# Attention heads in pairs: bias and mask added on VectorE with the maximum, scores four items ahead

## The reference

```python
def joint_softmax(parts, extra=None):
    m = parts[0].max(-1, keepdims=True)
    for p in parts[1:]:
        m = jnp.maximum(m, p.max(-1, keepdims=True))
    if extra is not None:
        m = jnp.maximum(m, extra)
    es = [jnp.exp(p - m) for p in parts]
    den = es[0].sum(-1, keepdims=True)
    for e in es[1:]:
        den = den + e.sum(-1, keepdims=True)
    if extra is not None:
        den = den + jnp.exp(extra - m)
    return [e / den for e in es]

def neighbourhood_attention(q, k, v, k_ctx, v_ctx, rpb):
    ...
    bias = jnp.where(col_ok[None, None, :, None, :], bias, NEG)
    s_loc = jnp.einsum('bhrqd,bhrjkd->bhrqjk', qg, kg, preferred_element_type=jnp.float32) * scale + bias
    s_ctx = jnp.einsum('bhrqd,bhld->bhrql', qg, k_ctx, preferred_element_type=jnp.float32) * scale
    p_loc, p_ctx = joint_softmax([s_loc.reshape(b, h, rows, GRID_W, kh * GRID_W), s_ctx])
    ...
    o = (jnp.einsum('bhrqjk,bhrjkd->bhrqd', p_loc, vg)
         + jnp.einsum('bhrql,bhld->bhrqd', p_ctx.astype(v.dtype), v_ctx))

def window_gqa(q, k, v, k_ctx, v_ctx, sink):
    ...
    ok = (jnp.abs(kpos - qpos) <= SWA_WINDOW) & (kpos >= 0) & (kpos < n)
    s_loc = jnp.where(ok, jnp.einsum('bkgnqd,bknmd->bkgnqm', qb, kb, preferred_element_type=jnp.float32) * scale, NEG)
    s_ctx = jnp.einsum('bkgnqd,bkld->bkgnql', qb, k_ctx, preferred_element_type=jnp.float32) * scale
    p_loc, p_ctx = joint_softmax([s_loc, s_ctx], extra)
    ...
```

## Time and profile before

| | us |
|---|---|
| median of three runs | 2750.54 |
| lowest and highest | 2749.99, 2753.0 |
| the profiled execution | 2752.89 |
| its span | 2751.1 |
| PE busy in the span | 2641.9 (96%) |
| DVE busy | 1401.4 (51%) |
| ACT busy | 571.7 (21%) |
| mean granted clock of TensorE | 0.983 |

### The profile page before, as it was taken

One profiled execution on the slowest core, in us unless ns is written; L12 is line 12 of the kernel. 1 busy time (PEld: TensorE's weight loads), 2 busy tenths in 40 slices (PEclk: granted clock), 3 DMA queues, 4 the chain that ended last, 5 costly groups with the idle time before them and its releaser, 6 DMA issues.

```text
span 2751.1 us, 38407 instructions
## 1 busy us (share of the span) xinstructions
PE 2641.9 (96%) x15510; PEld 1859.8 (68%) x15510; DVE 1401.4 (51%) x2718; ACT 571.7 (21%) x1142; POOL 545.3 (20%) x420
## 2 busy tenths in 40 slices
PE   7999999999999999999999999999999998999998
PEld 4347568888865655789964464788888756655554
DVE  2556366466758677533556542765555335410111
ACT  1215221100033334322022041100000225201110
POOL 0000034444400000047830000444454000000000
PEclk8999999999999999999999999999999998999998
DMA  8551035555333423445445400554543300499995
GB/s 299 199 185 53 31 124 199 182 179 175 110 86 99 115 74 100 152 151 179 144 128 208 145 31 32 177 188 163 168 142 113 124 1 1 171 417 412 415 404 219
DMA packets 218210, 446.71 MB, mean 162 GB/s; under 512 B 18762, under 2 KB 115849, under 8 KB 214955
## 3 DMA queue, kind: packets, MB, share of 16 engines
q1 hardware_dynamic: 176688, 329.78, 33.4%
q10 hardware_dynamic: 41338, 114.40, 12.3%
HBM read 443.01 MB, written 1.13 MB: 161 GB/s over the span
## 4 chain that ended last, share of the span: by engine, by line
PE 89%; DVE 5%; ACT 2%; DMA 1%; issue 1%; POOL 0%; SPq 0%; DVEq 0%; ACTq 0%; POOLq 0%
PE bank L1101 34%; PE bank L929 24%; PE bank L2955 5%; PE bank L953 4%; PE bank L945 3%; PE bank L2974 3%; PE bank_pair L2955 2%; PE bank L2464 1%; DMA slot<-in_ada_w 1%; PE bank L2991 1%; PE bank L2040 1%; PE bank_pair L2974 1%; PE bank L2033 1%; PE bank L2457 1%; PE bank L2928 1%
## 5 line engine op out<-in xcount | busy, mean ns | idle before, releaser
L1101 PE MATMUL bank<-arena,slot 128*128 128x256 f32 (+1 forms) x3704 | 677.0, 343 | 6.3 <-DVE arena L1081 2.9
L1101 PEld LDWEIGHTS bank<-arena,slot 128*128 128x128 f32 x3704 | 605.0, 191 | 70.5 <-issue 8.0
L1114 POOL TENSOR_TENSOR slot<-slot 128x512 f32<-128x512 f32 (+3 forms) x208 | 269.3, 1295 | 1578.5 <-PE bank L1101 699.6
L929 PE MATMUL bank<-uT,slot 128*128 128x512 f32 (+2 forms) x1312 | 484.8, 525 | 2.8 <-ACT arena L2073 2.8
L929 PEld LDWEIGHTS bank<-uT,slot 128*128 128x128 f32 (+1 forms) x1312 | 246.5, 190 | 217.2 <-issue 205.0
L1101 PE MATMUL bank<-uT,slot 128*128 128x256 f32 (+1 forms) x1728 | 335.4, 351 | 6.3 <-ACT uT L681 6.1
L1101 PEld LDWEIGHTS bank<-uT,slot 128*128 128x128 f32 x1728 | 290.7, 192 | 44.6 <-ACT uT L681 10.4
L1115 POOL TENSOR_TENSOR slot<-slot 128x512 f32<-128x512 f32 (+3 forms) x208 | 286.8, 1379 | 0.0
L929 PE MATMUL bank<-arena,slot 128*128 128x256 f32 (+1 forms) x576 | 185.2, 485 | 3.8 <-DVE arena L1762 2.3
L929 PEld LDWEIGHTS bank<-arena,slot 128*128 128x128 f32 x576 | 111.9, 195 | 75.8 <-issue 66.9
L650 DVE SCALAR_TENSOR_TENSOR arena<-arena 128x1024 f32<-128x1024 f32 x95 | 122.3, 1297 | 11.9 <-issue 8.8
(11 more groups left out here) (459 smaller groups left out, 3064.9 us busy)
## 6 DMA issues: line engine op xcount, KB each, us to landing
slot<-in_ffn_w SPq DMA_DIRECT2D x42, 2048.0 KB, 8.7
arena<-in_ada_wt ACTq DMA_DIRECT2D x100, 512.0 KB, 3.6
slot<-in_moe_w SPq DMA_DIRECT2D x62, 704.0 KB, 16.8
arena<-in_moe_w SPq DMA_DIRECT2D x52, 704.0 KB, 17.8
rstd<-in_ada_wt ACTq DMA_DIRECT2D x48, 512.0 KB, 3.6
slot<-in_moe_w SPq DMA_DIRECT2D x11, 2048.0 KB, 18.8
slot<-in_ssd_w_in SPq DMA_DIRECT2D x32, 512.0 KB, 6.9
uT<-in_ada_wt ACTq DMA_DIRECT2D x28, 512.0 KB, 3.6
```

What stands on the lines that cost most here:

```text
L929: ins = pe.matmul(bank[0:m, 0:t1 - t0], w[:, k, c0:c0 + m], x[:, k, t0:t1], start=(k == 0), stop=(k == kt - 1))
L1101: ins = pe.matmul(bank[:, u * n:u * n + n], a[:, k, u * P:u * P + P], x[:, k, :], start=(k == 0), stop=(k == self.h - 1))
L1114: pool.tensor_tensor(out[:, :, 0:c], x[:, :, 0:c], y[:, :, 0:c], op)
```

## The change

- **s**: bias and mask leave TensorE. `pair_pe` is now two products of all keys (L2436), in the two row halves. VectorE's `maximum` takes the maximum of the keys without bias (L2474), and one fused instruction (L2477, `tensor_tensor_reduce`) adds the bias to the first 256 scores in the bank, writes them back there, and goes on with the maximum. In the engine's list it is the main instruction and an accumulator's read, both named ISA.
- The probabilities are normalised before the transpose (`normalise`, L2464 to L2467): for single-map items VectorE multiplies them by the reciprocal of the sum in SBUF and gives the signal `pn`, on which t now waits.
- **o**: a pair's two items together (`outputs_pe`, L2447), weights the values (64 columns), the transposed probabilities streaming, the two items to the two halves of the output's partitions. The result has channels on partitions, so VectorE copies it once per pair to `m_y` (L2598), and **f** falls away for single-map items.
- Scores of single-map items are made four items ahead, two-map items two ahead as before; `m_s` grows to six tiles (`m_ps`), `m_pt` to four. ScalarE does an item's exponential ahead of the copy of the same step, for single-map items.

Cut to what matters:

```diff
...
-        m_pt = [uT[:, 4 + i, :] for i in range(2)]
+        m_ps = [uT[:, i, :] for i in range(4)] + [m_o[:, 0:512], m_o[:, 1024:1536]]
+        m_pt = [uT[:, 4 + i, :] for i in range(4)]
...
+            AHEAD = {1: 4, 2: 2}
+
+            def __init__(self, items, turns):
+                self.items, self.turns, self.steps = items, turns, range(-self.AHEAD[1], len(items) + 2)
                 self.maps = list(itertools.accumulate(len(it["maps"]) for it in items))
                 N, order = len(items), []
-                for n in range(-ahead, N + 2):
-                    for m in self.scored(n + ahead):
+                for n in self.steps:
...
-                    if 0 <= n - 1 < N:
+                    if 0 <= n - 1 < N and not (self.paired(n - 1) and n % 2):
...
+            def due(self, n):
+
+                for maps, ahead in self.AHEAD.items():
+                    m = n + ahead
+                    if 0 <= m < len(self.items) and self.paired(m) == (maps == 1):
+                        yield m
...
-                nk, biased = its[0]["nk"], its[0]["bias"] is not None
-                if biased:
-                    for it, bank in zip(its, banks):
-                        pe.matmul(bank[:, 0:LAT], ident, it["bias"], start=True, stop=False)
-                    for it, bank in zip(its, banks):
-                        q, k = it["maps"][0]
-                        pe.matmul(bank[:, 0:LAT], q, k[:, 0:LAT], start=False, stop=True)
-                at = LAT if biased else 0
                 for it, bank in zip(its, banks):
                     q, k = it["maps"][0]
-                    pe.matmul(bank[:, at:nk], q, k[:, at:nk], start=True, stop=True).then_inc(B.full_sem, 1)
+                    pe.matmul(bank[:, 0:it["nk"]], q, k, start=True, stop=True).then_inc(B.full_sem, 1)
+
+            def outputs_pe(self, pe, B, n):
+
+                its = self.items[n - 1:n + 1]
+                bank = B.empty(pe, self.order["o", n, 0])
+                for m in (n - 1, n):
+                    B.freed(pe, self.order["t", m, 0])
+                last = len(its[0]["v"]) - 1
+                for t in range(last + 1):
+                    for a, it in enumerate(its):
+                        ins = pe.matmul(bank[64 * a:64 * a + 64, 0:P], it["v"][t], m_pt[(n - 1 + a) % 4][:, t * P:t * P + P],
+                                        start=(t == 0), stop=(t == last))
+                ins.then_inc(B.full_sem, 1)
...
+            def normalise(self, dve, ch, pr, n):
+
+                it, (den, es, rc) = self.items[n], self.stats(n, 0)[2:5]
+                dve.wait_ge(*pr)
+                if it["sink"] is not None:
+                    dve_link(ch, dve.tensor_tensor(den, den, es, ALU.add))
+                dve_link(ch, dve.reciprocal(rc, den))
+                s = self.score(n, 0)
+                dve.tensor_scalar(s, s, rc, None, ALU.mult).then_inc(*S("pn").given())
+
+            def maximum(self, dve, ch, B, m, j):
+
+                it, (mx, nm) = self.items[m], self.stats(m, j)[0:2]
+                bank = B.full(dve, self.order["s", m, j])
+                at = 0 if it["bias"] is None else LAT
+                dve_link(ch, dve.tensor_reduce(mx, bank[:, at:it["nk"]], AX.X, ALU.max))
+                if at:
+                    s = bank[:, 0:at]
+                    dve_link(ch, dve.tensor_tensor_reduce(out=s, in0=s, in1=it["bias"], scale=1.0, scalar=mx, op0=ALU.add,
+                                                          op1=ALU.max, accum_out=mx))
+                if it["sink"] is not None:
+                    ins = dve.tensor_scalar(nm, mx, -0.125, sinks[:, 8 + it["sink"]:9 + it["sink"]], ALU.mult, ALU.min)
+                else:
+                    ins = dve.tensor_scalar(nm, mx, -0.125, None, ALU.mult)
+                ins.then_inc(*S("nm").given())
...
-                        two = len(it["maps"]) == 2
-                        pe.wait_ge(*S("pn" if two else "pr").taken("pe"))
-                        S("pr").passed("pe", 2 if two else 0)
+                        pe.wait_ge(*S("pn").taken("pe"))
...
             def act(self, act, B, ch):
+                    due = list(self.due(n))
+                    for m in due:
+                        if self.paired(m):
+                            self.probabilities(act, B, m)
                     if 0 <= n < N:
                     if 0 <= n < N:
+                        self.turned(act, B, n)
+                    for m in due:
+                        if not self.paired(m):
+                            self.probabilities(act, B, m)
...
             def dve(self, dve, B, ch):
+                for n in self.steps:
+                    due = list(self.due(n))
+                    for m in due:
+                        for j in range(len(self.items[m]["maps"])):
+                            self.maximum(dve, ch, B, m, j)
+                    for m in self.due(n - 1):
+                        if self.paired(m):
+                            self.normalise(dve, ch, (pr, before + self.maps[m]), m)
+                    for m in due:
+                        if not self.paired(m):
+                            self.combine(dve, ch, (pr, before + self.maps[m]), m)
+                    if ("o", n - 1, 0) in self.order:
...
+                        bank = B.full(dve, i)
                         if it["sub"]:
                             dve.wait_ge(*S("root").taken("dve"))
-                            rc = self.stats(n - 1, 1)[5]
+                            dve.tensor_scalar(it["o"], bank[:, 0:P], self.stats(n - 1, 1)[5], None, ALU.mult)\
+                               .then_inc(*B.free(i))
                         else:
-                            dve.wait_ge(pr, before + self.maps[n - 1])
-                            if it["sink"] is not None:
-                                dve_link(ch, dve.tensor_tensor(den, den, es, ALU.add))
-                            dve_link(ch, dve.reciprocal(rc, den))
-                        bank = B.full(dve, i)
-                        dve.tensor_scalar(it["o"], bank[:, 0:w], rc, None, ALU.mult).then_inc(*B.free(i))
+                            dve.tensor_copy(it["o"], bank[:, 0:P]).then_inc(*B.free(i))
...
-                        o=rows[:, t, h * 64:h * 64 + 64]))
-                if t == 3:
-                    n = len(items)
-                    turns[n - 1] = (m_y[:, 4 + f, :], [rows[:, t, f * P:f * P + P] for t in range(4)], None, range(n - 8, n))
-            return items, turns
+                        o=m_y[:, 4 + f, t * P:t * P + P]))
+            return items, {}
```

More of the change, by code:

```diff
@@ L2555, in even_attention @@
         def even_attention():
-            rows = m_o.rearrange("p (t c) -> p t c", t=4)
-            items, turns = [], {}
+            items = []
             for f, t in itertools.product(range(4), range(4)):
@@ L2583, in odd_attention @@
                         v=[m_v[:, j, 64 * (h // 4):64 * (h // 4) + 64] for j in range(4)],
[L2584 to L2587 removed]
+                        o=m_y[:, f, t * P:t * P + P]))
             for d, t in itertools.product(range(4), range(2)):
```

101 lines of the change are left out of this document (43 added, 58 removed).

## The result

The changed kernel takes 2758.14 us (median of 20 runs), the kernel before 2752.78 in the same comparison: a ratio of 1.0017, 95% interval 1.001 to 1.0023. One of the 20 runs took 5498.34 us, twice the others, and is not in the ratio. That is inside the 0.2% that the prediction counted as no change, but on the slow side of it, where a gain was forecast (2746.7), and the 2758.14 lie outside the forecast range, which ended at 2756.

The account below looks back on a forecast made before the run. TensorE bounds attention now; afterwards a loop through VectorE, ScalarE and TensorE would. Even stage -1.3 us and odd stage -2.5 make -3.8, from a median of 2750.54 to 2746.7 us; range 2736 to 2756, the forecast's own 2742 to 2751.

Parts of the forecast that it names:

- the sum of the two stages: Attention: even stage 58.9 us against 60.22 (-1.3), odd stage -2.5, together -3.8 us.
- TensorE gives up the bound, and its saving turns into waits: Attention stages: of TensorE's 30 us less work, 26 turn into waits for ScalarE's copies.
- "The order is" the bound, as a loop: Windowed heads: a round trip through VectorE, ScalarE and TensorE sets 4.23 us per odd pair, 13.6 per eight even items.
- the next bound below the loop: Rival, attention: waits overlap and VectorE's work bounds, 11.1 us per eight even items, 3.9 per odd pair; 2737 us, chance 0.16.
- So: 0.34, and 0.08 ... and 0.04, 0.46: VectorE's fused add and maximum, absent from the trace: 0.34 us, accumulator's read 0.08, link 0.04; instruction bounded above by 0.68.
- The dear rival: VectorE's fused instruction takes 0.68 us, +0.27 per odd loop and maximum (2.7 in all), +6.0 together: 2752.7 us, chance 0.14.
- The links: Handovers between engines in an odd pair's loop: scaling to ScalarE 0.19 us, copy to product 0.65, product to VectorE 1.15.
- The lead-in: Each stage's start, from VectorE's maxima and normalisations: item 5's scaling at 10.4 us odd, 8.5 even.
- granted clock 1.00 up to the two-map items: Sign that the forecast is right: TensorE keeps its full clock in attention until the odd stage's two-map items.
- the clock falls: Rival, paired heads: TensorE with gaps drops to 1.2 GHz; low for half the pairs gives +17 us, 2763; chance 0.10.
- The two-map part: End of the odd stage: VectorE bounds, loses add, reciprocal, scaling and the turn's copy, gains two copies: -1.7 us.
- No other stage is touched: Outside the two attention stages: the rest of the span moves only if the clock does.

Follow-up runs that it names:

- run 1: The changed kernel with ScalarE's copy of a turned tile ahead of the exponentials, the order of the kernel before: 2746.61 us, 0.9982 of the kernel before.
- run 9: The changed kernel with idle TensorE products, fewer than in an earlier trial, before the first transposes and value products of both attention stages: 2755.76 us, 1.0017.
- runs 1 and 2: run 1, and the changed kernel with bias and mask added by TensorE's identity products again and one maximum of 512 columns: 2756.23 us, 1.0015.
- run 11: The changed kernel timed again, unchanged, beside the kernel before: 2756.01 us, 1.0011.

## Why the prediction was wrong, point by point
The forecast span was 2751.1 - 3.8 = 2747.3, the profiled one is 2755.4. The 8.1 us between them: even stage +3.6 (62.48 against 58.9), odd windowed heads +3.8 (38.91 against 35.1), two-map part -1.1 (40.08 against 41.2), everything else +1.9. The structure was right and the sizes were not. The step that failed is the sum of the two stages: it priced the fused maximum at 0.46 us where it measures 0.58, the other links of a loop at 3.77 where they measure 3.91, and TensorE's clock in the lead-ins at nothing, where it cost 1.3 and 1.1 us.
- **TensorE gives up the bound, and its saving turns into waits: right.** Of 14 us less work in the even stage and 10 in the odd windowed heads nothing reached the total. 16 products in two column halves take 1.09 us and reach VectorE after 1.13; the forecast had 1.05 and 1.15. The Trainium skill (TensorE: Matmul & The Clock Gate, section Part 3: Packing small matmuls) would have them in line, over 3 us by the prediction's estimate; the measurement decides against it.
- **"The order is" the bound, as a loop: right**, and shown by run 1, which opens it with one exchange on ScalarE. It is also where the prediction stopped too soon: it named VectorE's work, 3.9 us a pair (4.11 by run 1), as the next bound below the loop, and did not ask whether the change's own new order on ScalarE was needed.
- **"So: 0.34, and 0.08 ... and 0.04, 0.46": the first mis-sized term.** The fused instruction takes 0.49 and its read 0.14; from its start to the scaling's start it is 0.58. I took the two-input row of 0.42 as nearest, and for the read the 83 ns of another instruction's. The bound of 0.68 held. This alone is +0.12 for each maximum on the path: five odd loops and six maxima ahead of them, 1.3 us in the odd stage, and, by the same estimate, about as much again in the even one. The dear rival put 0.27 on each maximum, so the forecast's price was a little nearer (0.12 too low against 0.15 too high). That rival's time, 2752.7, lies nearer to the measured one only because the other terms went the same way. Its "2.7 in all" is also too low: five loops and eight maxima at 0.27 make 3.5.
- **The links: mis-sized by 0.14 a loop.** 0.65 to the product is 0.75 (copy 0.60, then 0.15 and not the 0.05 of the earlier trace rows, where TensorE had waited 0.21 us and not 1.17), and 0.19 to ScalarE is 0.25; the others moved by 0.02 at most. With the fused instruction the loop is 4.50, not 4.23. The even group is 14.12, not 13.6: three of them make +1.6.
- **The lead-in was costed for VectorE alone.** Item 5's scaling came 11.4 us after the odd stage's start (10.4 forecast) and 9.0 after the even one's (8.5). What the sum left out altogether is TensorE's idling there, with the clock behind it. In the odd stage the loops from item 5 to 9 then took 5.3 and 5.0 us, not 4.5: 1.3 us more, 1.4 by run 9. In the even stage the same two loops took 8.6 us together, and 7.5 one group later: 1.1 more. The forecast's "granted clock 1.00 up to the two-map items" failed. So the odd windowed heads' 3.8 are 1.0 up to item 5, five loops of 0.26, 1.3 of clock and 0.2 behind the last scaling; the even stage's 3.6 are 0.5, three groups with 1.6, 1.1 of clock and 0.4 at the end.
- **The rival "the clock falls"** was set among the paired heads, where TensorE is two thirds busy. In the steady loops it did not fall: 1.00 in the windows of both stages, with transposes a good part of the work. By the rule of the Trainium skill that the prediction weighed (TensorE: Matmul & The Clock Gate, section Part 4: PE-mode transpose) it should have; these rows disagree with it as the earlier trace rows do. It fell at the stage's start, after the gaps, and stayed low into the first loops. The right mechanism stood in the wrong place and was left out of the sum of the likeliest case.
- **The two-map part**: -1.7 forecast, -2.8 measured. At the clock that runs 1 and 2 had there (0.88, near the 0.86 of before) it takes 41.4 us, -1.5: the term was right, and the other 1.4 are luck, from a clock of 0.96.
- **"No other stage is touched"**: true of the work, and yet 1.9 us came from there, 1.6 of them in the one line that run 11 shows, with its lower clock.
- **The range** ended at 2756. Its terms were spread one at a time, while three of them (instruction, links, lead-in) moved together and the same way.

## What to carry to other kernels
Before an engine is relieved, write down the loop that will bind next, and then try to break it in the order of the queues: one exchange on ScalarE was worth 10 us here, more than the 4 us forecast for the whole change, and splitting the bias between the two engines 3 us more. An instruction that no row shows is better taken with the middle of its bounds than with the lower one: here 0.51 and 0.12 for the read would have made 0.63, against 0.46 forecast and 0.58 measured. Its accumulator's read needs a price of its own. And count the lead-in of a stage on every engine: work taken off TensorE there left it idle here, and the clock it then got was paid for in the products that followed.

## What the runs showed of the hardware
- A fused add and maximum of 128x256 in PSUM takes 0.49 us and 0.14 for its accumulator's read; VectorE's reduce of the same columns 0.42, the read behind `scalar_tensor_tensor` 0.083.
- The granted clock fell with no gap of TensorE over 1.79 us before it (the even lead-in of the changed kernel), and the place of its fall moved with idle work elsewhere: run 9 has 1.00 in the odd lead-in and 0.89 in 2285 to 2300, where the changed kernel, with the same gap of 2.38 us before the same product, has 1.00.
- Sixteen products of 64 output rows in two column halves, with sixteen weight loads, take 1.09 us (L2447).
